# Two layers of a hybrid decoder on one core: the layer loop unrolled, conditioning groups of layer 1 computed in layer 0's attention loop

## The reference

```python
mod = (c @ w_ada_l + b_ada_l).reshape(c.shape[0], N_MOD, -1)          # 9 sequences, N_MOD = 9
sh1, sc1, gt1, sh2, sc2, gt2, sh3, sc3, gt3 = [mod[:, m][:, None, :] for m in range(N_MOD)]
f = swiglu(rms_norm(x, g[0]) * (1 + sc1) + sh1, w_gu[0], w_dn[0])
x = x + 0.5 * gt1 * rms_norm(f, g[1])
h = rms_norm(x, g[2]) * (1 + sc2) + sh2
xl, gl, q, k, v, qi, ki, wi = project(h, w_in_l, pos)
...                                     # RG-LRU on xl, gl; sparse attention (indexer, top-k, softmax) on the rest
y = jnp.concatenate([y_lru, y_att], axis=-1) @ w_o
x = x + gt2 * rms_norm(y, g[3])
f = swiglu(rms_norm(x, g[4]) * (1 + sc3) + sh3, w_gu[1], w_dn[1])
x = x + 0.5 * gt3 * rms_norm(f, g[5])
```

## Time and profile before

| | us |
|---|---|
| median of 3 runs | 3284.97 (3283.75 to 3287.01) |
| span of the profiled execution, the only time given for it | 3289.0 |
| TensorE busy | 2866.4 (87%) |
| VectorE busy | 1465.7 (45%) |
| ScalarE busy | 782.9 (24%) |
| conditioning matmuls L592, both layers | 307.7 |

### The profile page before, as it was taken

One profiled execution on the slowest core, in us unless ns is written; L12 is line 12 of the kernel. 1 busy time (PEld: TensorE's weight loads), 2 busy tenths in 40 slices (PEclk: granted clock), 3 DMA queues, 4 the chain that ended last, 5 costly groups with the idle time before them and its releaser, 6 DMA issues.

```text
span 3289.0 us, 56073 instructions
## 1 busy us (share of the span) xinstructions
PE 2866.4 (87%) x20506; PEld 2643.8 (80%) x20506; DVE 1465.7 (45%) x2006; ACT 782.9 (24%) x1076; POOL 158.8 (5%) x299
## 2 busy tenths in 40 slices
PE   5999997987778669999979999969796768699997
PEld 4999896976545669999969998969575548699997
DVE  2333124365799443332243331244648983533312
ACT  2233023220012133332223321222200122333221
POOL 0000001001320000000000000010113100000000
PEclk8999998975579789999989999989656888899998
DMA  6223632212353012322243226222123421123231
GB/s 183 82 85 89 176 88 79 73 43 61 112 148 109 26 39 83 89 85 74 87 123 89 84 82 186 85 72 75 48 69 110 146 86 40 42 85 89 69 88 62
DMA packets 524666, 291.09 MB, mean 89 GB/s; under 512 B 20673, under 2 KB 518882, under 8 KB 524162
## 3 DMA queue, kind: packets, MB, share of 16 engines
q1 hardware_dynamic: 513154, 266.35, 27.9%
q0 software_dynamic: 11392, 23.23, 2.4%
HBM read 285.75 MB, written 3.77 MB: 88 GB/s over the span
## 4 chain that ended last, share of the span: by engine, by line
PE 78%; DVE 7%; issue 6%; SPq 3%; DMA 2%; ACT 2%; DVEq 0%; POOL 0%; ACTq 0%; POOLq 0%
PE ps L581 19%; PE ps L583 19%; PE ps L582 19%; PE ps L703 4%; PE ps L592 4%; PE ps L553 3%; PE ps L701 3%; DMA sb_wslot<-w_ada 2%; PE ps L819 2%; SPq L433 2%; SPq L431 1%; PE ps L563 1%; ACT sb_h L864 1%; PE ps L723 1%; DVE sb_h L1149 1%
## 5 line engine op out<-in xcount | busy, mean ns | idle before, releaser
L582 PE MATMUL ps<-sb_h_lo,sb_w_hi 128*128 128x272 f32 x3360 | 974.4, 290 | 0.0
L581 PE MATMUL ps<-sb_h_hi,sb_w_hi 128*128 128x272 f32 x2816 | 818.7, 291 | 54.3 <-DVE sb_h_lo L1135 54.3
L583 PE MATMUL ps<-sb_h_hi,sb_w_lo_ffn 128*128 128x272 f32 x2816 | 820.8, 291 | 0.0
L874 ACT ACTIVATE sb_w_hi<-sb_wslot 128x1024 fp32r<-128x1024 f32 (+2 forms) x322 | 332.9, 1036 | 1485.9 <-PE ps L583 1337.0
L1110 DVE TENSOR_TENSOR sb_w_lo_ffn<-sb_wslot,sb_w_hi 128x1024 fp32r<-128x1024 f32 (+1 forms) x272 | 324.0, 1194 | 794.6 <-ACT sb_w_hi L874 794.0
L582 PEld LDWEIGHTS ps<-sb_h_lo,sb_w_hi 128*128 128x128 f32 x3360 | 642.3, 191 | 0.5
L581 PEld LDWEIGHTS ps<-sb_h_hi,sb_w_hi 128*128 128x128 f32 x2816 | 535.1, 190 | 59.4 <-issue 54.2
L583 PEld LDWEIGHTS ps<-sb_h_hi,sb_w_lo_ffn 128*128 128x128 f32 x2816 | 534.5, 190 | 0.0
L581 PE MATMUL ps<-sb_act_hi,sb_w_hi 128*128 128x272 f32 x1408 | 408.7, 290 | 11.1 <-DVE sb_w_lo_ffn L1110 11.1
L583 PE MATMUL ps<-sb_act_hi,sb_w_lo_ffn 128*128 128x272 f32 x1408 | 407.6, 290 | 0.0
L582 PE MATMUL ps<-sb_act_lo,sb_w_hi 128*128 128x272 f32 x1408 | 407.3, 289 | 0.0
(11 more groups left out here) (218 smaller groups left out, 3199.7 us busy)
## 6 DMA issues: line engine op xcount, KB each, us to landing
sb_wslot<-ffn_w_gu SPq DMA_DIRECT2D x176, 512.0 KB, 3.7
sb_wslot<-w_ada SPq DMA_DIRECT2D x144, 512.0 KB, 4.7
sb_wslot<-ffn_w_down SPq DMA_DIRECT2D x64, 512.0 KB, 3.9
sb_wslot<-w_in SPq DMA_DIRECT2D x32, 512.0 KB, 3.7
sb_wslot<-ffn_w_down SPq DMA_DIRECT2D x32, 384.0 KB, 3.4
sb_down<-key_pages POOLq DMA_DIRECT2D x128, 96.0 KB, 2.2
sb_down<-key_pages SPq DMA_DIRECT2D x128, 96.0 KB, 2.0
sb_wslot<-w_out SPq DMA_DIRECT2D x16, 512.0 KB, 3.9
```

The source lines that it names most:

```text
L581: mm(out, wh, xh, start=(kc == 0), stop=False)
L582: mm(out, wh, xl, start=False, stop=False)
L583: last = mm(out, wl, xh, start=False, stop=(kc == of - 1))
L874: act_fn(w_hi[s][:, 0:rows, 0:cols], wslot[i][:, 0:rows, 0:cols], ACT.Copy).then_inc(w_hi_done.sem, 1)
```

## The change

The outer loop of each engine is a Python loop now, so the code stands twice, once for each layer, and `l` is a number. The phases are made per layer. Layer 0 has groups 5 to 13 behind its FFN (5 to 8 of its own and 0 to 4 of layer 1), layer 1 has groups 14 to 17 (its own 5 to 8) and nothing at its start or in its first FFN. In the attention loop each step has two chunks in place of one (`CHUNKS`), until the layer's groups are used up: layer 0 has eight groups in its 32 steps, layer 1 four in its first 16. The ninth group of layer 0 is computed in the tail behind the loop. The bias of all groups is loaded once, as `bada`.

```diff
+CHUNKS = 2
+SPAN = DC // CHUNKS
+class Layer:
+    def __init__(self, l):
+        first = l == 0
+        self.ada0 = Phase(2 * RPF, RING, RING, is_ada=True) if first else None
+        self.gu1 = Phase(U_GU, RING, RING)
+        self.ada1 = Phase(3 * RPF, RING, RING, is_ada=True) if first else None
...
+        self.groups = range(l * NMOD + 5, min((l + 1) * NMOD + 5, DEPTH * NMOD))
+        self.ada = Phase(len(self.groups) * RPF, RING, RING, is_ada=True)
...
+        in_loop = min(len(self.groups), TILES * HEADS * CHUNKS // DC)
+        self.in_loop, self.in_tail = range(in_loop), range(in_loop, len(self.groups))
+        self.after_loop = [at for at in self.in_loop if SPAN * at + SPAN + 1 >= TILES * HEADS]
+    def chunks(self, n):
+        both = (divmod(c, DC) for c in range(n * CHUNKS, (n + 1) * CHUNKS))
+        return [(at, m) for at, m in both if at in self.in_loop]
+    def at_transposes(self, n):
+        return [at for at in self.in_loop if n == SPAN * at + SPAN + 1]
+    def at_bias(self, n):
+        return [at for at in self.in_loop if n == SPAN * at + SPAN + 2]
+    def at_half(self, n):
+        return [(at, half) for at in self.in_loop for half in range(2) if n == SPAN * at + (half + 1) * SPAN // 2]
...
@@ SyncE
+            sp.dma_start(bada[:, :, :], a["b_ada"]).then_inc(bada_full.sem, 16)
-            with sp.Fori(0, DEPTH) as l:
+            for l in range(DEPTH):
-                pieces(ADA2, ada, first=5 * DC, rounds=RPF)
+                ada_loads(L.ada, L.groups[0], 0, 1)
                 sp.wait_ge(kp_used[0].sem, kp_used[0].at(l, 4))
                 hold(sp, passed[0], kp_used[1].sem, kp_used[1].at(l, 4))
                 for n, s in enumerate(range(V_POOL, NSEQ)):
                     load_pages(sp, a["v_cache"], l, s * PAGES, 0, PAGES, vpage[s], vp_full[s])
-                    pieces(ADA2, ada, first=5 * DC, start=(n + 1) * RPF, rounds=RPF)
+                    ada_loads(L.ada, L.groups[n + 1], n + 1, 1)
+                ada_loads(L.ada, L.groups[4] if len(L.groups) > 4 else 0, 4, len(L.groups) - 4)
@@ TensorE, attention loop
-                    if hd == 0 and i:
-                        pe.wait_ge(yt_read.sem, yt_read.at(l, i - 1))
-                        ada_transposes(l, 5 + i - 1, 1)
-                    if hd == 4:
-                        pe.wait_ge(modT_ready.sem, modT_ready.at(l, 2 * (5 + i) + 1))
-                    ada_chunk(l, ADA2, i * RPF, hd, 0)
+                    for at in L.at_transposes(n):
+                        pe.wait_ge(ada_read.sem, ada_read.at(0, L.groups[at]))
+                        pe.wait_ge(yt_read.sem, yt_read.at(l, (n - 3) // HEADS))
+                        ada_transposes(0, L.groups[at], 1)
+                    for at, m in L.chunks(n):
+                        if m % RING == 0:
+                            pe.wait_ge(modT_ready.sem, modT_ready.at(0, 2 * L.groups[at] + m // RING))
+                        ada_chunk(0, L.ada, at * RPF, m, 0)
@@ TensorE, tail behind the loop
                 pe.wait_ge(t_read.sem, t_read.at(l, TILES * HEADS))
+                for at in L.in_tail:
+                    pe.wait_ge(yt_read.sem, yt_read.at(l, TILES))
+                    for m in range(DC):
+                        if m == RING:
+                            pe.wait_ge(ada_read.sem, ada_read.at(0, L.groups[at]))
+                        ada_chunk(0, L.ada, at * RPF, m, 1 - m // RING)
                 hold(pe, passed[1], exp_s.sem, exp_s.at(l, 1))
...
+                for at in L.in_tail:
+                    ada_transposes(0, L.groups[at], 1)
                 pe.wait_ge(sums.sem, sums.at(l, 1))
@@ VectorE
-                ada(ADA0, 0, 2)
+                if l == 0:
+                    hold(dve, passed[3], bada_full.sem, bada_full.at(0, 1))
+                    ada(L.ada0, 0, 2)
-                ffn_operands(0, GU1, DN1, lambda: ada(ADA1, 2, 5))
+                ffn_operands(0, L.gu1, L.dn1, lambda: ada(L.ada1, 2, 5) if l == 0 else None)
...
+                    for at in L.at_bias(n):
+                        ada_bias(L.groups[at] % NMOD, 1, L.groups[at] // NMOD)
+                    for at, half in L.at_half(n):
+                        ada_half(half, L.ada, at * RPF + half + 1, 0)
```

More of the change, by code:

```diff
@@ L323, in decoder @@
         s_in = sig("s_in", 0)
[L324 to L328, removed]
+        bada_full = sig("bada_full", 0, 16)
+        w_full = [sig(f"w_full{i}", 0, 16) for i in range(RING)]
+        ada_used = [sig(f"ada_used{i}", 0) for i in range(RING)]
+        w_hi_done = sig("w_hi_done", 0)
+        w_split = [sig(f"w_split{i}", 0) for i in range(RING)]
+        w_used = [sig(f"w_used{i}", 0) for i in range(2)]
         vec_full = sig("vec_full", 2, 16)
@@ L483, in pieces, with ada_loads @@
                             piece(ph, u, n, rows(src[:, :, bass.ds(u * (RING * P) + (first + n) * P, P)]))
+                def ada_loads(ph, group, start, groups):
+                    for n in range(groups):
+                        of, g = divmod(group + n, NMOD)
+                        pieces(ph, layer_of(a["w_ada"], of), first=g * DC - (start + n) * DC, start=(start + n) * RPF,
+                               rounds=RPF)
                 def ffn_loads(f, gu_ph, dn_ph, between):
@@ L637, in _ @@
             pe.wait_ge(cleared.sem, 1)
-            with pe.Fori(0, DEPTH) as l:
+            for l in range(DEPTH):
+                L = LAYERS[l]
                 l_[0] = l
-                ada(l, ADA0, 0, 2)
+                if l == 0:
+                    ada(l, L.ada0, 0, 2)
                 sums_of_squares(sq_ready, l, 0)
-                ffn(l, 0, GU1, DN1, lambda: ada(l, ADA1, 2, 5))
+                ffn(l, 0, L.gu1, L.dn1, lambda: ada(l, L.ada1, 2, 5) if l == 0 else None)
                 sums_of_squares(dn_read, l, 0)
@@ L872, in split @@
                 sc.wait_ge(w_used[s].sem, w_used[s].at(l_[0], m + ph.used0[s]))
-                rows = DN_K[n % len(DN_K)] if ph in (DN1, DN2) else DC
+                rows = DN_K[n % len(DN_K)] if len(DN_K) == ph.slots else DC
                 act_fn(w_hi[s][:, 0:rows, 0:cols], wslot[i][:, 0:rows, 0:cols], ACT.Copy).then_inc(w_hi_done.sem, 1)
@@ L925, in _ @@
             sc.wait_ge(eps_ready.sem, 1)
-            with sc.Fori(0, DEPTH) as l:
+            for l in range(DEPTH):
+                L = LAYERS[l]
                 l_[0] = l
@@ L936, in _ @@
                 for n in range(2):
-                    split(IN, 0, n)
+                    split(L.proj, 0, n)
                 root(l, 2)
@@ L1040, in _ @@
                 for n in range(2):
-                    split(OUT, 0, n)
+                    split(L.out, 0, n)
                 sc.wait_ge(kv_stored.sem, kv_stored.at(l, 3))
                 for n in range(DC):
-                    if OUT.has(0, n + 2):
-                        split(OUT, 0, n + 2)
-                    product_done(OUT, 0, n)
+                    if L.out.has(0, n + 2):
+                        split(L.out, 0, n + 2)
+                    product_done(L.out, 0, n)
                     act_fn(tok2(h[:, n, :]), halves(n % 2), ACT.Copy)
@@ L1061, in _ @@
             pool.wait_ge(s_in.sem, 64)
-            with pool.Fori(0, DEPTH) as l:
+            for l in range(DEPTH):
                 key_loads(pool, False, l, 0)
@@ L1089, in _ @@
             dve.wait_ge(s_in.sem, 64)
-            with dve.Fori(0, DEPTH) as l:
+            for l in range(DEPTH):
+                L = LAYERS[l]
                 st = Steps(dve, dve_step, DVE_STEPS, l, passed[3])
@@ L1211, in ada @@
                         for half in range(2):
-                            ada_half(g, half, ph, g * RPF + (half + 1 - first * RPF), half)
+                            ada_half(half, ph, g * RPF + (half + 1 - first * RPF), half)
                         ada_bias(g, 2)
@@ L1511, in _ @@
                 tile_output(TILES - 1)
-                ada_half(NMOD - 1, 1, ADA2, TILES * RPF, 0)
-                ada_bias(NMOD - 1, 0)
+                for at in L.after_loop:
+                    ada_half(1, L.ada, (at + 1) * RPF, 0)
+                    ada_bias(L.groups[at] % NMOD, 0, L.groups[at] // NMOD)
                 dve.wait_ge(mT_pe.sem, mT_pe.at(l, 1))
@@ L1528, in _ @@
                 v.tensor_reduce(mx3, sT3.rearrange("p s j c -> p s c j"), AX.X, ALU.max).then_inc(max_in.sem, 1)
+                for at in L.in_tail:
+                    ada_half(0, L.ada, at * RPF + 1, 1)
                 dve.wait_ge(pool_max.sem, pool_max.at(l, 1))
```

107 lines of the change are left out of this document (53 added, 54 removed).

## The result

The changed kernel takes 3306.54 us (median of 4 runs, 3303.63 to 3309.45) beside 3285.5 us for the kernel before on the same chip (4 runs, 3283.75 to 3287.01): a ratio of 1.0061, 95% interval 1.0047 to 1.0075. It is 0.6% (21 us) slower; forecast were 3323 us, 38 us slower.

A forecast was written before the change was run, and what follows sets the result against it. TensorE carries 78% of the wait chain but is held for w_ada tiles behind SyncE's 16-page blocks. -73.7 + 51 + 65 + 1 = +43 us, rounded down to +38 on 3284.97: 3323 us, range 3285 to 3352.

The forecast's parts named there:

- Turn and FFN: Layer 1's start and first FFN: removing groups 0 to 4 leaves the undisturbed chain, -27.5 and -46.2 us.
- the branch: Turn of the outer loop: VectorE's 5.53 us idle lies inside the 56.61 us and is not counted again.
- Block and latency: Attention loops: from a group's fourth chunk to the next group's first, behind 16 page issues, 27.15 us.
- The stretch of the first four chunks: TensorE, attention loops: start of a group's first chunk to end of its fourth, 13.5 us, then 14; bounds 9.5 to 17.8.
- Layer 0 from chunk 24 on: Rest of layer 0's attention loop, TensorE-bound: 8.3 us to step 14's mask, then 110 us.
- Layer 1, +51: Layer 1's attention loop, two chunks per step in steps 0 to 15: ends 52.0 us later, tail loses 1 us.
- Tail of layer 0: Behind layer 0's attention loop: eight chunks on TensorE hidden at 1.85 us each, 8 us late if slow; taken +0.5 us.
- the bias load: Before the first w_ada: loading the bias once adds one more issue, +0.4 us.
- the rounding down to +38: Total: +43 us lowered to +38, since most open bounds were said to have more room below than above.
- (first): Rival: static addresses make SyncE's pages 30% or more cheaper, no loss from 0.97 us; 13% with other near-zero outcomes.
- (second): Rival: TensorE stays slow or w_ada tiles come late under two chunks per step, 3360 us; 12%.
- The third: Rival: page blocks hold nothing back, stalls go (-16 us), layer 0 pays +14, total 3209 us; 5%.

The follow-up runs named there:

- experiment 3: Changed kernel with the conditioning groups put back where they were at one chunk per step, layers still unrolled, bias loaded once: 3272.7 us.
- experiment 8: Changed kernel with all value pages on GpSimd's queue, layer 1 at one chunk per step, layer 0's ninth group's transposes earlier: 3207.7 us.
- experiment 1: Changed kernel with all 128 value pages of a layer loaded by GpSimd's queue, none by SyncE: 3209.8 us.
- experiment 6: Changed kernel with the same 48 value pages per layer on SyncE, one behind each w_ada tile of later groups instead of 16 in a row: 3209.3 us.
- experiment 2: Kernel before the change, with all value pages on GpSimd's queue and nothing else altered: 3268.7 us.

## Why the prediction was right, and where its size was off

The mechanism came as told: three waits for w_ada of 14.0 to 16.4 us in each loop, at steps 4, 8 and 12, VectorE idle nearly as long, 29.1 us at the turn and 2.4 us ahead of the down weights. The size is a little over half of the 38 us forecast, by these terms:

- *Turn and FFN, -27.5 and -46.2:* measured -27.5 and -46.2. The undisturbed copies of the same chain, gave the length that was left. That the branch "adds nothing to the sum" holds, as it lies inside the 56.61; but experiment 3 shows that 7.0 us of it needed no group to be moved.
- *Block and latency, 27.15 us each:* from the end of the fourth chunk to the next group's first: 25.88, 27.62, 26.63 in layer 0 (914.32 - 888.44 and so on). A page takes 1.30 us (mean of the six blocks, 20.9 us by 16), and the assumption of 1 us less a block made it 1.31. This term was right, with some luck: the six blocks of the kernel before have a mean of 21.5 us, not the 21.85 of the row read, so that static addresses gave back 0.6 us a block and not 1. The prediction had no row that splits a page's issue; the trace of the kernel before does: 0.34 us are the transfer instruction (L433) and 0.27 the load of the page's number into a register (L431), and that load stays.
- *The stretch of the first four chunks, 13.5, 14 and 14 us: the term that was mis-sized.* Measured 9.35, 11.06 and 11.05 (879.09 to 888.44, 914.32 to 925.38, 953.00 to 964.05). The fast level of the clock is back sooner than I took. The windows of TensorE's clock behind the waits (busy time and count of PE, PEld, DVE, ACT, POOL; granted clock, DMA share, GB/s):

```profile
914.30:920.40 6.10, 6.08 (x33) 4.00 (x34) 0.00 (x0) 0.00 (x0) 2.57 (x5) 0.60 1.01 314
920.70:925.40 4.70, 4.70 (x45) 3.85 (x44) 2.72 (x5) 0.77 (x3) 1.61 (x3) 1.00 0.77 216
914.00:928.00 14.00, 13.68 (x99) 10.16 (x100) 5.30 (x8) 1.05 (x4) 5.37 (x10) 0.81 0.91 272
928.00:939.00 11.00, 7.77 (x60) 5.53 (x57) 10.91 (x15) 1.76 (x6) 4.30 (x8) 1.00 0.47 138
953.00:968.00 15.00, 14.99 (x112) 11.27 (x113) 6.75 (x11) 1.37 (x4) 0.00 (x0) 0.87 0.77 224
968.00:978.00 10.00, 7.92 (x62) 5.79 (x59) 9.41 (x11) 2.57 (x7) 0.00 (x0) 1.00 0.22 64
```

  After an idle time of 14 to 16 us the first pair of chunks takes 5.4 to 6.0 us, at a granted clock of 0.60 in the first window, so between the levels of 1.2 and 2.4 GHz; the second pair takes 3.66 us at 1.00, the fast level. I had let the slow level last through most of the stretch, as in the row at 900.39. The three stretches are 4.2, 2.9 and 3.0 us shorter than taken, together 10.0 us in layer 0, and the three times of block and latency 1.5: chunk 24 comes 111.6 us behind chunk 0, not 123.1.
- *Layer 0 from chunk 24 on:* forecast 118.3 us, measured 1105.57 - 990.68 = 114.9, and TensorE-bound as said: chunks 32 to 48 in 47.3 us (forecast 47.9), of which TensorE is busy 46.6. 11.5 + 3.4 make the 14.9 us between +65 and +50.2.
- *Layer 1, +51:* measured +42.8, for the same reason: chunk 24 comes 2596.55 - 2482.41 = 114.1 us behind chunk 0, not 123.1. Besides, the sum took layer 0's rows for layer 1, whose loop before is 1.7 us longer.
- *Tail of layer 0, +0.5:* measured +2.7 from the end of the loop to the first w_out product (1177.68 - 1105.57 = 72.1 us, was 1130.76 - 1061.33 = 69.4). The eight chunks on TensorE took 16.05 us and were hidden. 1.3 us are the bias add, which holds VectorE's last copy until all value products are done; experiment 8 undoes this. 1.9 us arise earlier, ahead of the first value product, and 0.5 are won back in that product, which takes 5.32 us and took 5.82. Of the 1.9 some 1.7 lie at the head of the tail, where VectorE waits for the prompt's last value products: ahead of them TensorE now has a pair of chunks (1105.40, 3.66 us) instead of one. VectorE before and after:

```profile
1064.22 0.20 DVE L1474 RECIPROCAL sb_arena<-sb_arena 128x8 f32<-128x8 f32 x1 [1.67 <-PE ps L767]
```

```profile
1110.13 0.20 DVE L1540 RECIPROCAL sb_arena<-sb_arena 128x8 f32<-128x8 f32 x1 [3.33 <-PE ps L819]
```

- *The sum:* -73.7 + 42.8 + 50.2 + 2.7 + 0.4 = +22.4 us, beside +21.0 in the medians and +38 forecast; the 0.4 for the bias load is the forecast's, no run shows it. The terms made +43, and the rounding down to +38 had no term behind it: that it went the right way is luck. The stretches came out near the fast bound of 9.5 us that the prediction gave them, and alone they make some 20 of the 22 us between +43 and +21.
- *Rivals:* pages take 1.30 us, not 0.97 (first). That point was itself misplaced: it counts the 38 us from 1.37 us a page, though the sum had already taken 1 us a block, so that the change would be no loss only at 0.91. TensorE went back to full clock and tiles weren't late but for the blocks (second). The third is what experiments 1 and 6 make of the kernel; its parts, -16 us for the stalls and +14 for the second chunk, are -17.3 and +17.1 in the loops of experiments 1 and 2.
- *The rule on issuing engines* (the Trainium skill, DMA: Bandwidth & Descriptors, "Issuing engines are not separate DMA queues"): it puts the gain of another issuing engine at the sequencer's issue time alone. The six blocks are 125 us of issue time, and experiment 1 gained 97. But experiment 6 gained as much with all that issue time left on SyncE: what counts is not how much issue time a queue has, but what stands behind it in the queue.

## What to carry to other kernels

In this kernel TensorE waited for whatever stood in SyncE's queue ahead of the next tile. Before the consumer of such a queue is made faster, compare the queue's longest run of other issues (here 21 us, 27 from the last free slot to the next tile's use) with what the buffers hold at the new rate (four tiles, two steps, 11 us), not with the mean rate. Here such waits added up one by one, and the cure was placement: one page behind each tile cost nothing where 16 in a row cost 15 to 17 us. Where a stage is removed, look for an undisturbed copy of the chain around it in the same trace, and read the remainder there.

## What the runs showed of the hardware

- On SyncE the transfer instruction itself takes 0.37 us for a w_ada tile of 512 KB and 0.34 for a page of 64 KB. From start to start, tiles with free slots are 0.65 us apart and pages 1.3. Between two pages stands the load of a page number into a register, 0.27 us (TENSOR_LOAD at L470), with register work around it. So here the price of an issue followed how its address is made, not its bytes.
- GpSimd issues the same pages every 1.40 us in the mean beside VectorE's loop (128 pages from 839.1 to 1017.2 us in experiment 1), most of them 1.27 to 1.34 us apart. With all 128 of a layer there (experiment 2), VectorE's steps without a wait are as long as before, 5.0 to 6.0 us.
- Behind each of the six waits of 14 to 16 us TensorE's first pair of chunks took 5.2 to 6.3 us and the second 3.66; the granted clock over the two pairs behind the first wait was 0.60 and 1.00.
